# Layer 0's rounds and the first out-projection in one program part, its first two tiles in one pass

## What is computed

```python
z = h_lat @ w_in                      # 1024 -> 4096: u, g, f, gf
u_l = centred_depthwise_conv(u_l, w_conv, b_conv)
r_l, r_c = rglru_bidirectional(u_l, u_c, w_a, b_a, w_x, b_x, lam)   # a scan forth, a scan back, summed
mix_l = concatenate([r_l * silu(g_l), fourier_mix(f_l, w_f, b_f) * silu(gf_l)])
y_lat = mix_l @ w_out                 # 2048 -> 1024, the same for the context
x = x + gate * rms_norm(y_lat, g_post)
# next: layer 1's h = rms_norm(x, g_pre) * (1 + scale) + shift, projections, windowed attention
```

## Time and profile before

| | us |
|---|---|
| median of 3 runs | 1520.12 (1519.18 to 1522.53) |
| the profiled execution | 1520.55 |
| its span, first to last instruction | 1518.8 |
| TensorE busy | 1389.6 (91%) |
| VectorE, ScalarE, GpSimd busy | 847.6, 737.3, 567.8 |
| mean granted TensorE clock | 0.969 |

### The profile page before, as it was taken

How to read it: one execution, slowest core, us unless ns; L and a number is a source line. 1 busy time by engine, 2 the same in 40 slices (tenths; PEclk the granted TensorE clock), 3 DMA queues, 4 the chain that set the end, 5 groups by cost and what they waited for, 6 DMA issues and landing times. The chain is left out here.

```text
span 1518.8 us, 20155 instructions
## 1 busy us (share of the span) xinstructions
PE 1389.6 (91%) x7212; PEld 1160.3 (76%) x7212; DVE 847.6 (56%) x1221; ACT 737.3 (49%) x1147; POOL 567.8 (37%) x268
## 2 busy tenths in 40 slices
PE   5999999999999999759999976999996899998897
PEld 4778888888888888637888855888885788887676
DVE  7788767677676867741111125122221789997532
ACT  5475828373646465442211213232221799998511
POOL 0023232322222233144434414334442566666542
PEclk9999999999999999979999987999998999999999
DMA  9313122212121212083443425634334533241584
GB/s 382 132 69 110 61 90 74 87 64 90 60 90 60 90 60 77 10 274 141 116 133 99 120 87 194 166 98 134 95 117 131 185 126 105 77 145 46 177 235 125
DMA packets 95285, 179.63 MB, mean 118 GB/s; under 512 B 10464, under 2 KB 57344, under 8 KB 92928
## 3 DMA queue, kind: packets, MB, share of 16 engines
q1 hardware_dynamic: 95232, 178.93, 36.6%
HBM read 123.84 MB, written 45.11 MB: 111 GB/s over the span
## 5 line engine op out<-in xcount | busy, mean ns | idle before, releaser
L880 PE MATMUL slab<-h_hi,w_hi 128*128 128x512 f32 x720 | 258.1, 358 | 3.2 <-DVE h_lo L279 2.6
L882 PE MATMUL slab<-h_hi,w_lo 128*128 128x512 f32 x720 | 257.3, 357 | 0.0
L881 PE MATMUL slab<-h_lo,w_hi 128*128 128x512 f32 x720 | 257.2, 357 | 0.0
L851 POOL TENSOR_TENSOR w_lo<-wraw,w_hi 128x1024 fp32r<-128x1024 f32 x29 | 73.8, 2545 | 311.4 <-ACT w_hi L517 311.4
L1877 POOL TENSOR_TENSOR probs<-probs,rdenom 128x2560 f32<-128x2560 f32 (+1 forms) x32 | 135.8, 4243 | 58.0 <-DVE rdenom L1836 58.0
L880 PEld LDWEIGHTS slab<-h_hi,w_hi 128*128 128x128 f32 x720 | 135.5, 188 | 25.9 <-DVE h_lo L279 2.9
L882 PEld LDWEIGHTS slab<-h_hi,w_lo 128*128 128x128 f32 x720 | 135.5, 188 | 22.1
L881 PEld LDWEIGHTS slab<-h_lo,w_hi 128*128 128x128 f32 x720 | 135.5, 188 | 22.0
L1557 PE MATMUL slab<-h_hi,w_hi 128*128 128x512 f32 (+1 forms) x352 | 135.6, 385 | 17.8 <-DVE h_lo L1479 17.8
L1287 PE MATMUL Y<-wo_hi,m_hi 128*128 128x512 f32 x320 | 128.1, 400 | 21.6 <-DVE wo_lo L1202 18.6
L1559 PE MATMUL slab<-h_hi,w_lo 128*128 128x512 f32 (+1 forms) x352 | 135.0, 383 | 0.0
(11 more groups left out here) (280 smaller groups left out, 3020.3 us busy)
## 6 DMA issues: line engine op xcount, KB each, us to landing
wraw<-in_w_in SPq DMA_DIRECT2D x32, 512.0 KB, 3.4
wm<-in_wm SPq DMA_DIRECT2D x32, 512.0 KB, 3.7
mixT<-work SPq DMA_DIRECT2D x16, 640.0 KB, 3.5
mraw<-mixT SPq DMA_DIRECT2D x20, 512.0 KB, 5.0
wm<-in_wm SPq DMA_DIRECT2D x8, 1024.0 KB, 15.9
q_parts<-qT SPq DMA_DIRECT2D x32, 256.0 KB, 4.6
oT<-o_out SPq DMA_DIRECT2D x8, 1024.0 KB, 5.3
work<-in_xT SPq DMA_DIRECT2D x8, 640.0 KB, 8.2
```

Source lines behind the costliest of these rows:

```text
L880: nc.tensor.matmul(out, l_hi, r_hi, start=start, stop=False)
L881: nc.tensor.matmul(out, l_hi, r_lo, start=False, stop=False)
L882: return nc.tensor.matmul(out, l_lo, r_hi, start=False, stop=stop)
```

## The change

One program part holds the rounds and the out-projection: no block end, barrier or clearing of semaphores stands between them (the clearing goes behind the out-projection; the few semaphores that layer 1 shares are cleared at the very end). The out-projection's tiles lie, by a hand-made layout, in memory of the rounds that has been used for the last time; each first write waits for the semaphore of that last use. Block numbers i below are places in `K_ORDER`, in which the scan's last row (k = 7) and the last Fourier row (k = 15) come last.

- Last round: ScalarE also makes the high parts of tiles 0 and 1 (first half of the mix without the last row) and of blocks 0 to 2; VectorE their low parts (GpSimd that of tile 0, and block 3's), blocks 4 and 5, and the sum of the two scan directions, which was GpSimd's.
- Eight slots for raw blocks instead of four. VectorE makes all low parts but that of block 3.
- The last scan row is split from `H` in SBUF for tiles 0 and 1 and not read back.
- Tiles 0 and 1 are made in one pass: the step of tile 1 follows that of tile 0 by three blocks. The transposes of the gate rows stand in the pass.
- Tile 2's product is cut in two halves, with tile 0's transposes between them and tile 1's behind. From tile 3 on the order is the old one.
- x has one buffer instead of two, loaded once the add of the tile before has read it.

The core of the diff:

```diff
+K_ORDER = [*range(KT - 1), *range(KT, K2 - 1), KT - 1, K2 - 1]
+LAG = 3
+RAW_SLOTS = 8
+POOL_LOW = 3
...
 # ScalarE, round t
-                if not last:
+                if last:
+                    mixed_hi(0, 0)
+                else:
                     split_hi(t + 1, SLAB_U)
                 root(t, 1)
-                tanh_g(t, (2,) if first else range(3))
+                if last:
+                    tanh_g(t, (0,))
+                    weight_hi(0)
+                    weight_hi(1)
+                    mixed_hi(1, 0)
+                    tanh_g(t, (1, 2))
+                    weight_hi(2)
...
 # VectorE, round t
+                if last:
+                    silu_g(0)
+                    weight_lo(0)
+                    silu_g(1)
+                    weight_lo(1)
+                    mixed_lo(1, 0)
+                    silu_g(2)
+                    weight_lo(2)
...
                 stt(out=xf[:], in0=xf[:], scalar=0.5, in1=sgf[:], op0=ALU.mult, op1=ALU.mult).then_inc(mf, 1)
+                if last:
+                    weight_lo(4)
+                    weight_lo(5)
+                    dve.wait_ge(hd, 2 * t + 2)
+                    tt(H[:], H[:], E[:, 0:T], ALU.add).then_inc(hs, 1)
                 dve.wait_ge(hs, t + 1)
...
 # SyncE, behind the last round's loads
+        sp.wait_ge(freed.mrs, 16 * (KT - 1))
+        load_first_mix(0, 0, 0)
+        load_first_mix(1, 0, 1)
+        sp.wait_ge(freed.s_gf, 3 * KT)
+        load_w(0)
+        load_w(1)
+        sp.wait_ge(freed.gate_products, 12 * KT)
+        load_w(2)
+        sp.wait_ge(freed.s_g, 3 * KT)
+        for i in range(3, 10):
+            load_w(i)
+        store_f()
+        load_w(10)
+        sp.wait_ge(freed.mfs, 16 * KT)
+        sp.wait_ge(m0l, 1)
+        sp.wait_ge(ml[0], 1)
+        load_first_mix(0, 1, 1)
+        load_first_mix(1, 1, 0)
+        load_w(11)
+        store_r()
+        load_w(12)
+        load_w(13)
+        store_gates()
+        load_w(14)
+        load_w(15)
+        sp.wait_ge(freed.gates_stored, 32)
+        sp.dma_start(gpb[:], a["gp"][0].partition_broadcast(P)).then_inc(par, 16)
+        load_x(0)
+        sp.wait_ge(freed.mrs, 16 * KT)
+        load_mix(2, 0)
+        load_mix(2, 1)
+
+        def body(t, s, last):
+            if not (isinstance(t, int) and t == 1) and not last:
+                load_mix(t + 1, 0)
+                load_mix(t + 1, 1)
+            load_x(t)
+            store(t - 1, 1 - s)
...
 # ScalarE, behind the rounds
+            for i in range(3, 7):
+                weight_hi(i)
+            mixed_hi(0, 1)
+            weight_hi(7)
+            mixed_hi(1, 1)
+            last_r()
+            for i in range(8, K2):
+                weight_hi(i)
+            act.wait_ge(es, 1)
+            loops(act, body)
+            epilogue(TT - 1, 1)
...
 # VectorE, behind the rounds
+            weight_lo(6)
+            mixed_lo(0, 1)
+            weight_lo(7)
+            mixed_lo(1, 1)
+            last_r()
+            for i in range(8, 12):
+                weight_lo(i)
+            copy_gates()
+            for i in range(12, K2):
+                weight_lo(i)
...
 # TensorE
+                if k == KT:
+                    pe.wait_ge(ml[1], t + 1)
+                elif k == KT - 1:
+                    pe.wait_ge(freed.r7_lo, t + 1)
+                if t == 0:
+                    low_ready(pe, i)
+                last = block(t, k, i == 0, i == K2 - 1)
...
+            for i in range(K2 + LAG):
+                if i < K2:
+                    step(0, i)
+                if i >= LAG:
+                    step(1, i - LAG)
+                if i == 8:
+                    gate_rows()
...
+        first_pair()
+        half_product(2, 0, 0)
+        transposes(0, 0)
+        half_product(2, 0, 1)
+        transposes(1, 1)
+        body(3, 1)
+        with pe.Fori(2, LT // 2) as j:
+            body(2 * j, 0)
+            body(2 * j + 1, 1)
```

More of the change, by code:

```diff
@@ L15 @@
 import numpy as np
+from collections import namedtuple
 from contextlib import ExitStack
@@ L133, in setup @@
     par = sem("par_loaded")
-    x_ld = [sem(f"x_loaded{i}") for i in range(KT)]
+    x_ld = [sem(f"x_then_wo_loaded{i}") for i in range(KT)]
     wm_ld = [sem(f"wm_loaded{i}") for i in range(WM_SLOTS)]
@@ L404, in mixers @@
         w_ld = [sem("w_loaded0"), sem("w_loaded1")]
-        set_sync, set_scalar, set_vector, set_tensor, hl, modk = before
+        set_sync, set_scalar, set_vector, set_tensor, hl, modk, slot_ld = before
         par = sem("mix_par_loaded")
@@ L497, in _, with store_f, store_r, store_gates @@
             loops(sp, body)
[L498 to L504, removed]
+            def store_f():
+                sp.wait_ge(mf, KT)
+                sp.dma_start(a["mixT"][2 * KT - 1], xf[:]).then_inc(mfs, 16)
+            def store_r():
+                sp.wait_ge(mr, KT)
+                sp.dma_start(a["mixT"][KT - 1], H[:]).then_inc(mrs, 16)
+            def store_gates():
+                sp.wait_ge(ge, 2)
+                for i in range(2):
+                    sp.dma_start(a["gp"][i].rearrange("w (k n) -> (w k) n", n=P), g_rows[:, i, :]).then_inc(gst, 16)
+            out_sync(sp, store_f, store_r, store_gates)
         @blk.scalar
@@ L812, in body @@
                 scan(1)
-                for c in (2,) if first else range(3):
-                    silu_g(c)
+                if last:
[6 more added lines that the diff above has]
+                    weight_lo(2)
+                else:
+                    for c in (2,) if first else range(3):
+                        silu_g(c)
                 dve.wait_ge(us, t + 1)
@@ L867, in body @@
                     split_lo(t + 1, SLAB_U)
-                pool.wait_ge(hd, 2 * t + 2)
-                sub(H[:], H[:], E[:, 0:T], ALU.add).then_inc(hs, 1)
+                if not last:
+                    pool.wait_ge(hd, 2 * t + 2)
+                    sub(H[:], H[:], E[:, 0:T], ALU.add).then_inc(hs, 1)
             pool.wait_ge(modk, KT)
@@ new lines, in vector, with gpsimd, split, epilogue @@
+        return weight_lo, mixed_lo, rest
+    def gpsimd(pool):
+        tt = nc.gpsimd.tensor_tensor
+        def split(t, s, h):
+            pool.wait_ge(mh[h], t + 1)
+            tt(m_lo[s][:, h], mraw[:, h], v32(m_hi[s][:, h]), ALU.subtract).then_inc(ml[h], 1)
+        def epilogue(t, s):
+            w = 1 if is_ctx(t) else 0
+            pool.wait_ge(x_ld, 16 * t + 16)
+            pool.wait_ge(yn, t + 1)
+            tt(x1[:, s, :], x1[:, s, :], xt[:], ALU.add).then_inc(xd, 1)
+            pool.wait_ge(hg, t + 1)
+            tt(hb[:, s], hb[:, s], mods[:, SHIFT1, w, :].unsqueeze(2).to_broadcast([P, KT, P]), ALU.add).then_inc(hd, 1)
+        def body(t, s, last):
+            if not last:
+                split(t + 1, 1 - s, 0)
+                split(t + 1, 1 - s, 1)
+            epilogue(t - 1, 1 - s)
+        pool.wait_ge(mh[0], 1)
+        tt(m_lo[0][:, 0, 0:KT - 1], mraw[:, 0, 0:KT - 1], v32(m_hi[0][:, 0, 0:KT - 1]), ALU.subtract).then_inc(m0l, 1)
+        pool.wait_ge(woh, POOL_LOW + 1)
+        tt(wo_lo[POOL_LOW], wr[POOL_LOW], v32(wo_hi[POOL_LOW]), ALU.subtract).then_inc(wolp, 1)
+        loops(pool, body)
```

569 lines of the change are left out of this document (315 added, 254 removed).

## The result

| | before | after |
|---|---|---|
| median of four runs | 1520.53 us (1519.18 to 1522.53) | 1508.35 us (1503.66 to 1509.24) |
| profiled execution, its span | 1520.55, 1518.8 us | 1508.78, 1507.0 us |
| mean granted clock | 0.969 | 0.974 |

The ratio of after to before is 0.9917, with a 95% interval of 0.9898 to 0.9936: 12 us faster. The forecast was 1507.3 with a range of 1500 to 1515. The marks on TensorE's timeline of the kernel after stand beside those of the earlier trace rows; the last field is the idle time ahead and what ended it.

What follows compares the result with a forecast made beforehand. TensorE work bounds the kernel, so time can be gained only at the seam between layer 0's rounds and out-projection. Terms -16.7 + 1.8 + 2.0 = -12.9 us give 1507.6, stated as 1507.3 for the median; range 1500 to 1515.

Steps and rivals of the forecast that it cites:

- Start of the pass: Between layer 0's rounds and out-projection: tile 0 starts at 637.4 to 638.0 at full clock, and 23 us go.
- Supply of the first blocks: In the pass over tiles 0 and 1: TensorE waits 0.7 us for GpSimd's block 3; L829 ends at 643.5.
- The starved second half: In the pass at block 7: store lands at 649.1, TensorE stands 4.4 us, clock dip 2.3, end at 689.6.
- Wait for Y: Behind the pass: tile 2 waits 1.5 us for tile 0's scaled row; tile 0's transposes start at 702.0.
- The new wait: Ahead of tile 1's transposes: a chain of 20.5 us stalls TensorE 8.6 us; low clock behind it costs 1.8.
- Rival 1: The chain is no bound at tile 1, which gives back 8.6 + 1.8 us: 1497; chance 0.08.
- The period behind it: Out-projection behind tile 1's transposes: the period stays the old one, 22.67 us a tile.
- Boundary: Semaphore clearing behind the out-projection and at the very end: 1.0 us each, 2.0 in all (0.5 to 4).
- Sum: Whole kernel: tile 1's transposes -16.7, clock +1.8, semaphore clearing +2.0, together -12.9 us; forecast 1507.3, chance 0.70.
- rival 2: The pass starves longer: block 7 is ready 5.7 us later and the dip costs its full 3.1: 1514; chance 0.14.
- rival 3: The pass starts only after the modulation columns, near 645, 7.6 us more: 1515; chance 0.03.
- Rival 4: The clock stays at 1.2 GHz through the pass, which takes 80.6 us: 1543, slower than before; chance 0.05.

## Why the prediction was right, and where its steps were not

- **Start of the pass.** Forecast 637.4 to 638.0 at full clock; measured 636.73. The splits in the last round fill idle time there, as said. That they are the cause is shown by the two versions without them, where TensorE waits 6.69 us first.
- **Supply of the first blocks.** Wait for GpSimd's block: forecast 0.7, measured 0.34. L829's operation (now L900) beside GpSimd's subtraction took 2.15 us, from 640.57, while GpSimd's ran 2.41 from 638.96 and ended at 641.37; the forecast end of 643.5 was 642.7. One GpSimd operation costs its overlap, not the sum of both. The Trainium skill (SBUF — State Buffer, "SBUF: two separate sides") says that one of the two holds the shared ports and the other blocks. The trace agrees: 641.37 plus VectorE's own 1.45 is 642.8.
- **The starved second half.** Forecast: store issued 643.6, landed 649.1, wait 4.4, clock dip 2.3, pass ends 689.6. Measured: 642.75, 649.49, 4.51, a low clock in 657 to 663 that put 13 matmuls 0.43 instead of 0.233 us apart (2.5 us), and an end at 689.4. The cause is shown by moving the store ahead. The other executions of this queue order with paired tiles and early splits waited 2.14 to 3.47, so the forecast of 4.4 was at the late end of what happens, and its agreement with the profiled execution is luck in part; the prediction took the landing from one rate (359 GB/s) and gave it no spread of its own to the early side.
- **Wait for Y.** Forecast 1.5, measured none. The step counted three steps of tile 1 behind tile 0's last one; the trace shows four (683.99 to 689.4), since with a lag of three tile 1's step of the same turn comes behind tile 0's too. The chain of 5.6 us was right: the last product of tile 0 ends near 684.0 and its scaled row at 688.25 + 1.28 = 689.5. Counted properly, tile 0's transposes were to come at 700.5, measured 700.95.
- **The new wait.** Forecast 20.5 us of chain and a stall of 8.6; measured 20.38 and 8.32, and 20.31 to 20.35 in the five other executions that keep its order. The clock behind it cost 24.78 - 23.09 = 1.7 (forecast 1.8; 1.4 to 2.8 in the other versions). Taking the mix load out of the chain gave 8.0 back. Rival 1 (the chain binds nothing) falls.
- **The period behind it.** "From there the period is the old one" is the step that failed: 23.09 instead of 22.67, six periods to tile 8, 2.5 us. The prediction took the matmul's spacing as fixed by its shape; the trace shows that it changes with where its operands lie, and the change moved all of them.
- **Boundary.** Forecast 2.0 at two places; measured 1.5 at the first (4.61 against 3.10; SyncE now waits 1.4 us for TensorE's queue there, at L83 behind the clearing) and nothing at the end of the kernel, where it is 605.4 us before and 605.3 after from the next stage's first load to the end.
- **Sum.** -17.8 (forecast -16.7), +2.1 (1.8), +2.5 (0), +1.5 - 0.1 (2.0): -11.8 against -12.9. The nearness is luck in part, since misses cancel: the period, 2.5 too little, against 1.1 too much in the first term (the Y wait that didn't come, in the main) and 0.6 too much at the boundary.
- **Rivals.** The pass did not starve longer (rival 2), it started where said (rival 3). Rival 4 needed 30 us at the low level; the two dips of the kernel after lasted about 7 us each (656.6 to 663.4 and 718.0 to 724.8). The Trainium skill (TensorE: Matmul & The Clock Gate, "HAM oscillation") has a loop fall back to the low level at each wait. The prediction let that stand for the longer waits alone. The runs have the fall after shorter ones too, of 2.14 and 2.66 us, but not after each wait: after 1.06, 1.12, 1.90 and 1.91 us the clock stayed up.

## What to carry to other kernels

When work is drawn ahead into a gap, follow each chain that the gap used to cover, in the order of the queues: here the new order left half a product over a chain of 20 us, and a single load issued one store earlier gave 8 us of it back. A store on which a load depends should be issued ahead of bulk loads of the same queue that are not wanted sooner, and such repairs set what earlier work ahead of them is worth: the early splits were worth 3 to 5 us in the median with the starved pass, 11.5 (7.4 by the traces) without. After moving matmul operands, compare the spacing of matmuls in a stretch without waits; a few nanoseconds each count where they are most of the kernel.

## What the runs showed of the hardware that was not expected

- Matmuls of one shape (128x128 by 512 columns, fp32r) at full clock with no wait between them were 0.2267 or 0.2333 us apart, 3%, depending on the memory that holds the moving weights. Behind a change from the slow to the fast place the first nine still took 0.231. The place is shown; what in it decides is open.
- A store of 0.66 MB that a load waits for took 3.48 and 3.50 us to release it with four weight loads issued ahead of it, and 4.66 to 6.74 with seven (six executions). The two versions without the early splits are left out, since SyncE's other waits differ there.
- The granted clock fell to 0.50 after a TensorE wait of 2.14 us that ended at 656.24: it was 1.00 during the wait, 0.73 in 656 to 658 and 0.50 in 658 to 660, with the engine at work. Waits of 1.06, 1.12, 1.90 and 1.91 us brought no drop.
- With one more clearing of semaphores and a meeting of all engines between two program parts, SyncE's path there was 1.5 us longer (4.61 against 3.10), 1.4 of it a wait at L83. No run takes the clearing alone out.
